# The gate products of a recurrent layer: whole fp32 in place of three rounded products

## The reference

```
def rglru_mixer(h, w_in, conv_w, conv_b, w_a, b_a, w_x, b_x, lam, w_out):
    proj = h @ w_in
    xr, gate = proj[..., :LRU_WIDTH], proj[..., LRU_WIDTH:]
    ...                                     # xc: xr convolved over 4 tokens, with bias
    xblk = xc.reshape(B, S, LRU_BLOCKS, LRU_BLOCK_W)
    r = sigmoid(einsum('bsnw,nwv->bsnv', xblk, w_a) + b_a)
    i = sigmoid(einsum('bsnw,nwv->bsnv', xblk, w_x) + b_x)
    log_a = -LRU_C * r * softplus(-lam)
    a = exp(log_a)
    u = sqrt(-expm1(2.0 * log_a)) * (i * xc)
    ...                                     # state = a * state + u over the tokens
    return (hs * silu(gate)) @ w_out
```

## Time and profile before

| what | value |
|---|---|
| median of three runs | 930.55 us |
| the profiled execution | 929.42 us, span 927.6 us, mean granted clock 0.975 |
| PE busy over the span | 854.4 us, 92% |
| DVE busy | 718.8 us, 77% |
| ACT busy | 514.1 us, 55% |
| POOL busy | 85.7 us, 9% |

### The profile page before, as it was taken

How to read it: one execution, slowest core, us unless ns; L and a number is a source line. 1 busy time by engine, 2 the same in 40 slices (tenths; PEclk the granted TensorE clock), 3 DMA queues, 4 the chain that set the end, 5 groups by cost and what they waited for, 6 DMA issues and landing times.

```text
span 927.6 us, 14747 instructions
## 1 busy us (share of the span) xinstructions
PE 854.4 (92%) x5661; PEld 777.5 (84%) x5661; DVE 718.8 (77%) x1124; ACT 514.1 (55%) x885; POOL 85.7 (9%) x123
## 2 busy tenths in 40 slices
PE   2889899999999999999999999999788999999886
PEld 2667678999999989999788999999678999878874
DVE  4755978887888769789878887766778767788886
ACT  2223757545454466458473455545465767766783
POOL 3100110010000000023000031100000000000120
PEclk9989899999999999999999999999799999999998
DMA  9987684688798657986856889896454674547431
GB/s 319 339 265 269 227 251 161 208 277 303 284 332 296 215 194 258 379 311 213 315 160 248 304 249 270 265 265 217 136 160 137 226 273 159 159 133 231 137 136 46
DMA packets 124997, 216.29 MB, mean 233 GB/s; under 512 B 12507, under 2 KB 98247, under 8 KB 118784
## 3 DMA queue, kind: packets, MB, share of 16 engines
q1 hardware_dynamic: 108300, 133.74, 43.8%
q0 software_dynamic: 13808, 73.51, 23.0%
q10 hardware_dynamic: 2820, 8.11, 2.6%
HBM read 214.18 MB, written 1.15 MB: 232 GB/s over the span
## 4 chain that ended last, share of the span: by engine, by line
PE 62%; DVE 17%; ACT 10%; DMA 6%; issue 4%; POOL 0%; DVEq 0%; ACTq 0%; POOLq 0%
PE bank L579 11%; PE bank L580 11%; PE bank L581 11%; PE bank L585 7%; PE bank L587 7%; PE bank L586 7%; DMA modraw<-in_mod_w 6%; DVE w_lo L1646 3%; DVE modsum L1678 3%; ACT w_hi L1127 2%; ACT kk L1189 1%; PE bank L705 1%; PE bank L855 1%; DVE kk L2238 1%; DVE x L1743 1%
## 5 line engine op out<-in xcount | busy, mean ns | idle before, releaser
L579 PE MATMUL bank<-h_hi,w_hi 128*128 128x256 f32 x1144 | 330.3, 289 | 15.6 <-DVE h_lo L1790 9.2
L1646 DVE TENSOR_TENSOR w_lo<-raw,w_hi 128x1024 fp32r<-128x1024 f32 (+1 forms) x236 | 278.1, 1215 | 64.2 <-ACT w_hi L1127 63.8
L580 PE MATMUL bank<-h_lo,w_hi 128*128 128x256 f32 x1144 | 326.2, 285 | 0.0
L581 PE MATMUL bank<-h_hi,w_lo 128*128 128x256 f32 x1144 | 326.0, 285 | 0.0
L1127 ACT ACTIVATE w_hi<-raw 128x1024 fp32r<-128x1024 f32 (+1 forms) x236 | 238.1, 1036 | 75.1 <-PE bank L581 29.2
L579 PEld LDWEIGHTS bank<-h_hi,w_hi 128*128 128x128 f32 x1144 | 220.9, 193 | 21.0 <-issue 15.2
L580 PEld LDWEIGHTS bank<-h_lo,w_hi 128*128 128x128 f32 x1144 | 221.1, 193 | 1.5 <-issue 0.5
L581 PEld LDWEIGHTS bank<-h_hi,w_lo 128*128 128x128 f32 x1144 | 220.8, 193 | 0.4
L585 PE MATMUL bank<-w_hi,o_hi 128*128 128x512 f32 x304 | 121.7, 400 | 1.5 <-DVE o_lo L2179 0.8
L587 PE MATMUL bank<-w_hi,o_lo 128*128 128x512 f32 x304 | 118.6, 390 | 0.0
L586 PE MATMUL bank<-w_lo,o_hi 128*128 128x512 f32 x304 | 118.5, 390 | 0.0
(11 more groups left out here) (296 smaller groups left out, 1178.8 us busy)
## 6 DMA issues: line engine op xcount, KB each, us to landing
raw<-in_ffn_w_in SPq DMA_DIRECT2D x88, 512.0 KB, 6.4
modraw<-in_mod_w POOLq DMA_DIRECT2D x32, 1024.0 KB, 6.5
raw<-in_ffn_w_out SPq DMA_DIRECT2D x44, 512.0 KB, 7.3
modraw<-in_ada_w POOLq DMA_DIRECT2D x16, 1024.0 KB, 5.5
raw<-in_attn_w_in SPq DMA_DIRECT2D x26, 512.0 KB, 5.4
raw<-in_moba_w_in SPq DMA_DIRECT2D x24, 512.0 KB, 9.8
modraw<-in_mod_w POOLq DMA_DIRECT2D x20, 512.0 KB, 5.3
modraw<-in_ada_w POOLq DMA_DIRECT2D x16, 512.0 KB, 5.1
```

The source lines that it names most:

```text
L579: pe.matmul(dst, cut(hi(u)), a_hi, start=first, stop=False, skip_group_check=True)
L580: pe.matmul(dst, cut(hi(u)), a_lo, start=False, stop=False, skip_group_check=True)
L581: return pe.matmul(dst, cut(lo(u)), a_hi, start=False, stop=last, skip_group_check=True)
L1646: dve.tensor_tensor(lo(v), raw_unit(v), hi(v).bitcast(F32), ALU.subtract).then_inc(sem("w_lo_ready"), 1)
```

## The change

The four wax units are no longer split. A set `whole` names the units that are multiplied as they land, and `split[u]` counts the split units up to u, so that the semaphores of the others still count right. `gates` makes one fp32 product per block from the convolved tile in `kk` and the landed weights in `raw`, in place of three. It waits tile by tile for the convolution itself (`xc_full`), and so does POOL. The rounding and the rest of the convolved tiles (`branch_high`, `xc_low`) are gone. In `free_chunk` a wax chunk is now free when PE has used it. The diff, cut to its changed lines and one line around them, without the one in `beside_units` that writes `split0` out:

```diff
--- before.py
+++ after.py
@@ -400,10 +400,11 @@
 
-        split0 = unit0("mla_o", 0)
+        whole = set(range(unit0("mla_o", 0))) | {unit0("wax", i) + j for i in range(2) for j in range(2)}
+        split = [sum(v not in whole for v in range(u + 1)) for u in range(NU)]
 
         beside_units = {
             "moba": {t: unit0("moba_in", 9) + t for t in range(6)} | {t: unit0("moba_o", 0) + t - 6 for t in range(6, 10)},
@@ -472,10 +473,11 @@
             def free_chunk(n):
-                if 2 * (n - RAW) < split0:
-                    sp.wait_ge(sem("w_used"), 2 * (n - RAW) + 2)
+                last = 2 * (n - RAW) + 1
+                if last in whole:
+                    sp.wait_ge(sem("w_used"), last + 1)
                 else:
-                    sp.wait_ge(sem("w_lo_ready"), 2 * (n - RAW) + 2 - split0)
+                    sp.wait_ge(sem("w_lo_ready"), split[last])
 
@@ -558,7 +560,7 @@
                 pool.wait_ge(sem("rg_read"), 8 * i + 8)
-                pool.wait_ge(sem("xc_ready"), 2 * i + 2)
+                pool.wait_ge(sem("xc_full"), 4 * i + 4)
                 pool.tensor_tensor(tiles(vv, 4 * i, 4 * i + 4), tiles(vv, 4 * i, 4 * i + 4),
@@ -568,8 +570,8 @@
             def start_unit(u):
-                pe.wait_ge(sem("w_hi_ready"), u + 1 - split0)
-                pe.wait_ge(sem("w_lo_ready"), u + 1 - split0)
+                pe.wait_ge(sem("w_hi_ready"), split[u])
+                pe.wait_ge(sem("w_lo_ready"), split[u])
 
@@ -1083,14 +1085,14 @@
                     u = unit0("wax", i) + j
-                    start_unit(u)
+                    start_whole(u)
                     for k in range(4):
                         n = 4 * i + k
-                        if j == 0 and k % 2 == 0:
-                            pe.wait_ge(sem("xc_ready"), n // 2 + 1)
-                        ins = feature_product(bank[gate_banks[i][j][k // 2]][:, (k % 2) * S:(k % 2 + 1) * S], u,
-                                              lambda r: r[:, k * P:(k + 1) * P], tiles(o_hi, n, n + 1),
-                                              tiles(o_lo, n, n + 1), True, True)
+                        if j == 0:
+                            pe.wait_ge(sem("xc_full"), n + 1)
+                        ins = pe.matmul(bank[gate_banks[i][j][k // 2]][:, (k % 2) * S:(k % 2 + 1) * S],
+                                        raw_unit(u)[:, k * P:(k + 1) * P], tiles(kk, n, n + 1), start=True, stop=True,
+                                        skip_group_check=True)
                     ins.then_inc(sem("w_used"), 1)
@@ -1115,17 +1117,19 @@
         def _(act):
-            nxt = [split0]
+            nxt = [0]
 
...
                     v = nxt[0]
+                    nxt[0] += 1
+                    if v in whole:
+                        continue
                     act.wait_ge(sem(f"w_in{v // 2 % RAW}_{v % 2}"), landed[v // 2])
-                    if v >= split0 + UNITS:
+                    if split[v] > UNITS:
                         act.wait_ge(sem("w_used"), v - UNITS + 1)
                     act.activation(hi(v), raw_unit(v), ACT.Copy).then_inc(sem("w_hi_ready"), 1)
-                    nxt[0] += 1
 
@@ -1556,10 +1560,6 @@
 
-            def branch_high(m):
-                act.wait_ge(sem("xc_full"), 2 * m + 2)
-                act.activation(tiles(o_hi, 2 * m, 2 * m + 2), tiles(kk, 2 * m, 2 * m + 2), ACT.Copy).then_inc(
-                    sem("xc_hi"), 1)
             def decay(i):
@@ -1596,15 +1596,12 @@
                 first_taps(m)
-                branch_high(m)
             ahead(unit0("l_gate", 0) + AHEAD)
...
             first_taps(2)
-            branch_high(2)
             first_taps(3)
             input_root(0)
-            branch_high(3)
             ahead(unit0("l_gate", 1) + AHEAD)
@@ -1627,7 +1624,7 @@
         def _(dve):
-            nxt, mod_n, fold_n, chain = [split0], [0], [0], [0]
+            nxt, mod_n, fold_n, chain = [0], [0], [0], [0]
 
@@ -1642,10 +1639,12 @@
                     v = nxt[0]
-                    dve.wait_ge(sem("w_hi_ready"), v + 1 - split0)
+                    nxt[0] += 1
+                    if v in whole:
+                        continue
+                    dve.wait_ge(sem("w_hi_ready"), split[v])
                     dve.tensor_tensor(lo(v), raw_unit(v), hi(v).bitcast(F32), ALU.subtract).then_inc(
                         sem("w_lo_ready"), 1)
-                    nxt[0] += 1
 
@@ -2218,12 +2217,6 @@
 
-            def xc_low(m):
-                dve.wait_ge(sem("xc_hi"), m + 1)
-                dve.tensor_tensor(tiles(o_lo, 2 * m, 2 * m + 2), tiles(kk, 2 * m, 2 * m + 2),
-                                  tiles(o_hi, 2 * m, 2 * m + 2).bitcast(F32), ALU.subtract).then_inc(
-                                      sem("xc_ready"), 1)
-
             def branch(m):
@@ -2277,18 +2270,14 @@
             branch(1)
-            xc_low(0)
             ahead(unit0("xr", 1) + 1 + AHEAD)
             modulate(1)
-            xc_low(1)
             ahead(unit0("l_gate", 0) + AHEAD)
...
             ratio(0)
-            xc_low(2)
             ahead(unit0("xr", 2) + 1 + AHEAD)
             branch(3)
-            xc_low(3)
             ahead(unit0("xr", 3) + 1 + AHEAD)
...
             scans(0)
```

More of the change, by code:

```diff
@@ L401, in build @@
                        for n, key in enumerate(turn_keys)}
-        split0 = unit0("mla_o", 0)
+        whole = set(range(unit0("mla_o", 0))) | {unit0("wax", i) + j for i in range(2) for j in range(2)}
+        split = [sum(v not in whole for v in range(u + 1)) for u in range(NU)]
         beside_units = {
-            "mla": {t: split0 + t + 1 - AHEAD for t in range(-1, 9)},
+            "mla": {t: unit0("mla_o", 0) + t + 1 - AHEAD for t in range(-1, 9)},
             "moba": {t: unit0("moba_in", 9) + t for t in range(6)} | {t: unit0("moba_o", 0) + t - 6 for t in range(6, 10)},
```

## The result

The changed kernel takes 933.37 us (median of 17 runs, 930.38 to 937.02) where the kernel before takes 929.21 us (17 runs, 926.86 to 931.62). The ratio is 1.0052, 95% interval 1.0039 to 1.0064: slower by 0.5%, some 4.8 us. Forecast were +3.5 us (0.38%) and a range of 930.5 to 937.0.

A forecast was written before the change was run, and what follows sets the result against it. ACT was taken to bound the stage through its splits ahead of both sigmoid groups. 3.4 us from the second late load plus 0.1 of clock gave 3.5, on the median of 930.55: 934.0 us, range 930.5 to 937.0.

The forecast's parts named there:

- What bounds the stage: Recurrent layer's gate stage: PE waits for DVE, DVE for ACT; ACT's splits ahead of both sigmoid groups count.
- Cost of a product: Gate products on PE: whole fp32 0.445 us against 0.36 for three rounded, so 0.7 us more per group.
- First gates: First gate group: PE gains 1.6 us, l_gate 1 load issued 3.6 us later, lands in 3.7, ACT's split 3.3 late.
- Given back between the groups: Between first and second gates: removed work nearly pays back the first delay; second gates start 0.6 us late.
- Second gates: Second gate group: lru_o 0 load issued 3.4 us later, lands in 3.68; nothing behind it swallows the delay.
- Rival 1: After the second gates: hidden slack gives back up to 1.8 us, leaving +1.6 to +2.6, no change; chance 0.26.
- The clock: PE's half-clock stretches after its waits: between nothing and 2.4 us, taken as 0.1 us.
- Rival 3: Half clock falls on the gates and lru_o: +2.4 us on top, 936.4, up to 937.5; chance 0.15.
- Rival 2: ACT need not wait for the landing, first sigmoid 2.7 us early: -3.3 us, 927.2, faster; chance 0.07.
- The number: Whole kernel: 3.5 us added to the three-run median of 930.55, giving 934.0 us, 0.38% slower.

The follow-up runs named there:

- e8: Changed kernel with each of the 16 gate products issued twice; ratio 1.0120 against the kernel before.
- e5: Changed kernel with ACT taking the sigmoids before the split of the late-loaded unit, in the first group only; ratio 1.0001 against the kernel before.
- e3: Changed kernel with ACT taking the eight sigmoids before the split of the late-loaded unit, in both groups; ratio 0.9973 against the kernel before.
- e4: Changed kernel with unread products in PE's waits, 24 ahead of xr 3 and 28 ahead of the output product; ratio 1.0041 against the kernel before.
- e2: Changed kernel with ACT copying each wax unit to a spare tile, so the ring place is freed early; ratio 0.9977 against the kernel before.
- e0: The changed kernel timed and profiled again, nothing altered; ratio 1.0051 against the kernel before.
- e6: Changed kernel with ACT taking the sigmoids before the split of the late-loaded unit, in the second group only; ratio 1.0012 against the kernel before.
- e11: Changed kernel with 30 unread products in PE's wait ahead of the output product alone; ratio 1.0036 against the kernel before.
- e1_hold: Kernel before, split products kept, with only the loads behind the wax chunks made to wait for PE's use; ratio 1.0077 against the kernel before.
- e9_before_later: Kernel before with only ACT's order changed, sigmoids ahead of the split of the next load's unit; ratio 1.0026 against the kernel before.

## Why the prediction was right, and where its sizes were off

- *What bounds the stage.* Right. ACT is the thread, and the two splits ahead of the sigmoids are the places.
- *Cost of a product.* Right: 3.62 us of records for eight, as worked out from the earlier trace rows. The four passes that the Trainium skill counts (FP8 and Floating Point Precision, section TensorE Precision Notes) would have given 3.84 at the measured step; the trace does not bear that out. That PE's length matters through the loads which it frees was in the sum; e8 shows it.
- *First gates.* The order of events is as forecast, and the load is issued 3.65 us behind the start of the gates. Mis-sized was the landing: 4.53 us in place of 3.7. Less the 2.1 us between the traces, ACT's split is 4.1 us late, not 3.3.
- *Given back between the groups.* The bookkeeping held: the second gates 1.5 us late instead of 0.6, 0.8 of the difference being the landing. But the sentence that the first delay "has nearly been paid back here" misleads, and what I expected of e5 from it (that the change's +4 to +5 us stay) was refuted. What paid was the removed work, which would have brought the second gates forward: to 41.9 us in e3, 3.3 us ahead of before. The first wait did not vanish, it ate a gain; e5 prices it at 4.6 us.
- *Second gates.* The load was forecast 3.4 us late and was 4.2 us late on the common scale, with a landing of 3.77 us (3.68 taken). The output product starts 4.3 us late, so nothing behind it swallowed the delay. Rival 1, absorption, is out.
- *The clock.* The term that was mis-sized most, at least in the profiles. Taken were 0.1 us, between bounds of 0 and 2.4; the two profiles show 2.0 and 1.7 us between output product and end. I allowed 0.9 there, from one slow unit of 4.4 us in the trace of before less the slack at 906.59; here half clock lasted 6 us and the slack did not show. The half clock behind the wait ahead of xr 3 cost little: in e4, where unread products fill this wait, the second gates start at 46.3 us, in the changed kernel at 46.7. Rival 3 was partly right beside the forecast, not in its place: the gates of the changed kernel ran at full clock. In the profile the layer is 6.3 us longer, 4.3 of waits and 2.0 of clock; the median of many executions has 4.2 to 4.8.
- *Rival 2*, the shorter path wins: its mechanism is real and its condition was not met. e3 meets it, e2 nearly, and they come out 2 to 2.5 us faster than before; the rival had 3.3.
- *The number.* 934.0 us forecast and 933.37 measured lie closer than the sizes do, which is luck: the forecast counts from 930.55, the median of three runs, and 17 runs of the kernel before give 929.21. The step itself was forecast at 3.5 us and measured at 4.2 (difference of medians) to 4.8 (ratio).

The landing of l_gate 1 has a reading, not isolated by a run. DVE, rid of `w_lo` and `xc_low`, sums a modulation part earlier, and POOL issues its next 512 KB earlier: in the changed kernel 2.4 us ahead of the load of l_gate 1, before the change 2.7 us behind it.

```profile
846.72 0.54 POOL L512 DMA_DIRECT2D modraw<-in_ada_w  x1 [5.35 <-DVE modsum L1677]
```

```profile
850.40 0.54 POOL L510 DMA_DIRECT2D modraw<-in_ada_w  x1 [6.28 <-DVE modsum L1678]
```

The first row is of the changed kernel, the second of the one before. The other runs fit: the same load takes 4.11 to 4.81 us in e0, e4, e5, e6 and e11, with POOL's load 2.4 us ahead in each, 3.38 us in e1_hold with 3.9 us between them, and 3.51 us in e8 with 5.9.

## What to carry to other kernels

When an operand is used where it landed instead of being copied on, its place in the ring is held until the last product: look up which load waits for that place, and who waits for that load in order. An in-order engine that prepares operands far ahead should do so behind the work that others wait for, since a late transfer in front of it costs most of its length: here waits of 6.07 and 4.31 us cost about 4.6 and 3.6. Where no transfer is late the same order is no gain; it lost 2.4 us in e9_before_later. Work taken off a path is worth something only once the new wait has been moved away; here 4.8 us slower and 2.5 us faster differ in the order of ACT's work alone.

## What the runs showed of the chip that I had not expected

TensorE's clock stayed at half for 6 us of the output product behind a wait of 4.27 us, and a stretch of half clock there cost up to 2.0 us; filling the wait with unread products kept it at full in three kernels of three.

The length of a wait did not tell by itself whether the clock falls. The 2.14 us inside the first gates left it at full in the trace of before; in e1_hold and e9_before_later the same 2.14 us were followed by some 3 us at 0.50. Ahead of unit 1 of l_gate 1 the clock fell behind 2.51 us before the change, and stayed at 1.00 behind 2.50 us in e3 and 3.17 us in e2.

The Trainium skill (TensorE: Matmul & The Clock Gate, section HAM oscillation) says that an array which waits between bursts falls back to half rate. The traces agree at the waits of 4.27 us, and at the shorter ones only in part.

A subtraction of DVE (a `w_lo`) and a multiplication of POOL, both of 128x1024, were both longer when they ran at once. DVE's took 3.37 us in place of 1.22 beside POOL's in e9_before_later, and POOL's took 5.77 us in place of 3.38 beside three of DVE's in the second half of the kernel before.
